# A two-layer diffusion backbone: opening reordered with part of the later keys moved in, last tile split

## The reference

```python
shift, scale, gate = adaln(c, ada_w[i], ada_b[i])        # silu(c) @ ada_w + ada_b, for c and c_ctx
h = rmsnorm(x, norm_w[i]) * (1.0 + scale) + shift         # the same for the context
# layer 0: gated linear attention, 4 heads of 256 keys and 512 values, chunked, in both directions
q, k, v, g = split(h @ w_in, [1024, 2048, 4096])          # 1024 + 1024 + 2048 + 2048 columns
la = log_sigmoid((h @ gate_a1) @ gate_a2 + gate_b) / 16   # decay, for each direction
y = (rmsnorm(o) * silu(g)) @ w_out
# layer 1: differential softmax attention, 8 heads, rotary positions, same shape of gate and output
x = x + gate * y
```

## Time and profile before

| | |
|---|---|
| median of 3 runs | 1578.0 us |
| profiled execution | 1577.87 us, span 1575.9 us |
| TensorE busy | 1545.3 us, 98%, 7602 matmuls |
| VectorE busy | 1161.7 us, 74% |
| ScalarE busy | 607.5 us, 39% |
| TensorE idle in 0 to 180 us, longest | 10.1 (first vectors), 4.7 (context rows), 2.0 (quad 4), 1.7 (remainder of k-tile 4), 1.2 (first w_lo) |
| TensorE idle in 160 to 1576 us | six waits of 0.8 us or less |

### The profile page before, as it was taken

How to read it: one execution, slowest core, us unless ns; L and a number is a source line. 1 busy time by engine, 2 the same in 40 slices (tenths; PEclk the granted TensorE clock), 3 DMA queues, 4 the chain that set the end, 5 groups by cost and what they waited for, 6 DMA issues and landing times.

```text
span 1575.9 us, 19506 instructions
## 1 busy us (share of the span) xinstructions
PE 1545.3 (98%) x7602; PEld 1251.7 (79%) x7602; DVE 1161.7 (74%) x1799; ACT 607.5 (39%) x934; POOL 2.2 (0%) x9
## 2 busy tenths in 40 slices
PE   5999999999999999999999999999999999999998
PEld 3567888788888878888878788888888888888886
DVE  4544878887787789677887787768676868676865
ACT  4222444433444434542232454333343424343642
POOL 0000000000000000000000000000000000000000
PEclk9999999999999999999999999999999999999999
DMA  9996444544544364345776354545445454252554
GB/s 332 363 371 205 131 138 124 186 157 121 168 135 154 113 216 160 108 127 154 251 256 214 95 166 149 177 154 175 143 138 159 136 172 147 94 174 81 162 177 143
DMA packets 177352, 269.02 MB, mean 171 GB/s; under 512 B 12534, under 2 KB 111024, under 8 KB 176588
## 3 DMA queue, kind: packets, MB, share of 16 engines
q1 hardware_dynamic: 170464, 256.55, 51.5%
q10 hardware_dynamic: 6796, 11.22, 2.1%
HBM read 265.60 MB, written 2.12 MB: 170 GB/s over the span
## 4 chain that ended last, share of the span: by engine, by line
PE 87%; DVE 6%; DMA 4%; issue 1%; ACT 1%; SPq 0%; ACTq 0%; DVEq 0%
PE bank L1175 68%; PE bank L1637 5%; DMA ada_w<-in_ada_w 3%; DVE ada_w L1690 3%; PE bank L1351 2%; PE bank L1107 2%; PE bank L1260 1%; PE bank L1261 1%; PE bank L1262 1%; DVE w_lo L1665 1%; DMA u<-in_ctx 1%; PE bank L1407 1%; PE bank L1408 1%; PE bank L1409 1%; PE bank L1589 1%
## 5 line engine op out<-in xcount | busy, mean ns | idle before, releaser
L1175 PE MATMUL bank<-w_lo,acts_hi 128*128 128x512 f32 x1536 | 605.6, 394 | 2.3 <-DVE work L2059 0.8
L1175 PE MATMUL bank<-w_hi,acts_lo 128*128 128x512 f32 x1536 | 598.4, 390 | 0.0
L1175 PE MATMUL bank<-w_hi,acts_hi 128*128 128x512 f32 x1536 | 598.2, 389 | 0.0
L642 ACT ACTIVATE w_hi<-w_raw 128x1024 fp32r<-128x1024 f32 (+1 forms) x296 | 304.7, 1034 | 619.3 <-PE bank L1175 535.5
L1665 DVE TENSOR_TENSOR w_lo<-w_raw,w_hi 128x1024 fp32r<-128x1024 f32 (+1 forms) x296 | 349.8, 1191 | 171.3 <-ACT w_hi L642 170.9
L1175 PEld LDWEIGHTS bank<-w_lo,acts_hi 128*128 128x128 f32 x1536 | 288.4, 188 | 72.7 <-issue 10.2
L1175 PEld LDWEIGHTS bank<-w_hi,acts_lo 128*128 128x128 f32 x1536 | 288.3, 188 | 60.6
L1175 PEld LDWEIGHTS bank<-w_hi,acts_hi 128*128 128x128 f32 x1536 | 288.6, 188 | 57.2
L1690 DVE SCALAR_TENSOR_TENSOR ada_w<-ada_w,silu_p 128x1024 f32<-128x1024 f32 x210 | 261.4, 1280 | 41.0 <-DMA ada_w<-in_ada_w 38.0
L1175 PE MATMUL bank<-acts_hi,w_lo 128*128 128x512 f32 x208 | 83.5, 402 | 2.9 <-DVE acts_lo L1790 1.7
L1175 PE MATMUL bank<-acts_lo,w_hi 128*128 128x512 f32 x208 | 81.6, 392 | 0.0
(11 more groups left out here) (227 smaller groups left out, 1511.1 us busy)
## 6 DMA issues: line engine op xcount, KB each, us to landing
ada_w<-in_ada_w SPq DMA_DIRECT2D x144, 512.0 KB, 4.4
w_raw<-in_diff_w_in SPq DMA_DIRECT2D x256, 256.0 KB, 3.1
w_raw<-in_gla_w_in SPq DMA_DIRECT2D x64, 512.0 KB, 4.3
u<-in_ada_w SPq DMA_DIRECT2D x32, 512.0 KB, 9.6
w_raw<-in_gla_w_out SPq DMA_DIRECT2D x32, 512.0 KB, 4.5
w_raw<-in_diff_w_out SPq DMA_DIRECT2D x32, 512.0 KB, 4.8
w_raw<-in_gla_w_in SPq DMA_DIRECT2D x40, 256.0 KB, 4.0
w_raw<-in_gla_w_in SPq DMA_DIRECT2D x48, 128.0 KB, 3.5
```

Source lines behind the costliest of these rows:

```text
L642: act.activation(w_hi[:, s, :, 0:w], raw[:, s, :, 0:w], ACT.Copy).then_inc(w_hi_ok, 1)
L1175: last = pe.matmul(bank[b][:], a, w, start=(k == 0 and i == 0), stop=(k == NK - 1 and i == 2))
```

## The change

1. Quads 2, 6 and 3 lie in the upper half of `acts_lo` (k-tiles 8 to 15), which is written later, and no longer in `raw`.
2. Pair (0,0) is loaded behind quad 3 and waits for no quad's use. Pairs of the OPEN keys follow behind quad 8. Two new pairs, EARLY, 384 columns wide, follow behind quads 10 and 11: the other key tile of heads 1 to 3, for k-tiles 0 to 3.
3. TensorE's list has a new order: the inverse RMS row ahead of quad 2, the first sum ahead of quad 4, both halves of pair 0 ahead of quads 6 and 7, pair 1 behind quad 8, `early_keys` (3 x 12 products) between quads 13 and 16, `gate_columns` later. VectorE does `low(0, 0)` inside `first_group(0)` and `low(0, 1)` behind `first_group(1)`.
4. The 36 products of `early_keys` are left out of heads 1 to 3: tile 2 of their first chunks starts at k-tile 4, pairs 0 and 1 are 256 columns wide, and VectorE adds the kept part to the result in place of copying it. VectorE copies the three parts out of PSUM, ScalarE moves them to `u`, and one is moved twice.
5. The last pair of weights does tile 0 first, then tile 1. VectorE handles the last tile in two halves of 256 columns; tile 0 and the second half are stored from ScalarE's queue, the first half from SyncE's.

```diff
@@ buffers
-        quad_slot = [ada_w[:, 0], ada_w[:, 1], raw_quads[:, 4:8]] + [u_quads[:, t] for t in range(NT)]
-        quad_slot.append(raw_quads[:, 0:4])
+        lo_quads = nc.alloc_sbuf_tensor_at("lo_quads", [P, 8, CW], F32, offset=lo_at + 4 * 8 * TOK)
+        quad_slot = [ada_w[:, 0], ada_w[:, 1], lo_quads[:, 0:4]] + [u_quads[:, t] for t in range(NT)]
+        quad_slot.append(lo_quads[:, 4:8])
@@ SyncE
-            BEHIND = {5: (0, 0), 7: (0, 1), 9: (OPEN, 0), 10: (OPEN, 1), 13: (0, 2), 14: (0, 3),
+            BEHIND = {3: [(0, 0)], 7: [(0, 1)], 8: [(OPEN, 0), (OPEN, 1)], 10: [(EARLY, 0)], 11: [(EARLY, 1)],
+                      15: [(0, 2)], 16: [(0, 3)], 17: [(OPEN, 2)], 18: [(OPEN, 3)], 20: [(0, 4)], 22: [(0, 5)],
...
-                    if p == 0:
-                        sp.wait_ge(ada_used, 4 if c == 0 else 7)
@@ ScalarE
             group_rows(0)
+            split(0, 0)
             first_highs(0)
-            split(0, 0)
...
                 splits(OPEN, range(2 * g - 2, 2 * g))
+                if g == 1:
+                    splits(EARLY, range(EARLY_PAIRS))
...
+            act.wait_ge(early_out, OPEN_TILES)
+            for i in range(OPEN_TILES):
+                act.activation(early_kept[i], early_part[:, i], ACT.Copy).then_inc(early_copied, 1)
@@ TensorE, project_pair
+                        first = 2 * EARLY_PAIRS if later_head(c) and t == 2 else 0
+                        if k < first:
+                            continue
@@ TensorE, new
+            def early_keys(i):
...
+                b, x = bank[(4, 5, 4)[i]], slice(i * P, (i + 1) * P)
+                for p in range(EARLY_PAIRS):
...
+                    for j in range(2):
...
+                        pe.matmul(b[:], wl, hi[:, k, :], start=(k == 0), stop=False)
+                        pe.matmul(b[:], wh, hi[:, k, :], start=False, stop=False)
+                        last = pe.matmul(b[:], wh, lo[:, k, :], start=False, stop=(k == 2 * EARLY_PAIRS - 1))
@@ TensorE, list of the opening
-            startup_quads(2, 4)
+            inverse_rms_row()
+            startup_quads(2, 3)
             lambda_sums()
-            inverse_rms_row()
+            startup_quads(3, 4)
+            gate_weight_transposes()
+            startup_sum(0)
             startup_quads(4, 5)
-            startup_sum(0)
-            gate_weight_transposes()
+            first_pair(0, range(1))
             startup_quads(5, 6)
-            first_pair(0, range(1))
+            first_pair(0, range(1, 2))
             startup_quads(6, 8)
             startup_sum(1)
-            first_pair(0, range(1, 2))
             startup_quads(8, 9)
-            first_pair(1, range(1))
+            first_pair(1)
             startup_quads(9, 10)
-            first_pair(1, range(1, 2))
             later_keys(0, 0)
-            startup_quads(10, 12)
+            startup_quads(10, 11)
             later_keys(0, 1)
-            gate_columns(range(0, 2))
-            startup_quads(12, 14)
+            startup_quads(11, 12)
             later_keys(0, 2)
+            startup_quads(12, 13)
+            early_keys(0)
+            startup_quads(13, 14)
+            early_keys(1)
             startup_quads(14, 16)
-            gate_columns(range(2, 4))
             startup_sum(2)
+            early_keys(2)
             startup_quads(16, 17)
             first_pair(2)
...
-            gate_columns(range(4, 6))
+            gate_columns(range(0, 4))
...
-            gate_columns(range(6, 8))
+            gate_columns(range(4, 8))
@@ VectorE, first_group
+                if g == 0:
+                    low(0, 0)
                 first_remainder(last)
@@ VectorE, list of the opening
             first_group(0)
-            low(0, 0)
             rows_scaled(range(4, 8))
-            low(0, 1)
-            first_group(1)
-            rows_scaled(range(8, 12))
-            low(OPEN, 0)
-            rows_scaled(range(12, NK))
...
+            rows_scaled(range(8, 10))
+            first_group(1)
+            low(0, 1)
+            rows_scaled(range(10, NK))
+            lows(OPEN, range(2))
             keys_partly(0, 0)
             keys_partly(0, 1)
+            lows(EARLY, range(EARLY_PAIRS))
+            keys_partly(0, 2)
+            early_partly(0)
+            early_partly(1)
             lows(0, range(2, 4))
             first_group(2)
-            keys_partly(0, 2)
+            early_partly(2)
@@ VectorE, heads 1 to 3
+                    elif not first and t == 2:
+                        kept = qkT[:, t] if h == G_HEADS - 1 else early_kept[h - 1]
+                        dve.tensor_tensor(qkT[:, t], bank[t][:], kept, ALU.add).then_inc(freed[t], 1)
@@ tail: TensorE and VectorE
+            def last_output_pair():
...
+                for t in range(2):
...
+                    last.then_inc(acc_ok if t == 0 else last_half, 1)
...
+                for n, (t, first, cols) in enumerate(((0, 0, CW), (1, 0, CW // 2), (1, CW // 2, CW // 2))):
```

More of the change, by code:

```diff
@@ L127, with later_head, width, pieces @@
 ACT_TILES = (9, 11, 13, 15)
-OPEN = -1
+OPEN, EARLY = -1, -2
 OPEN_TILES = G_HEADS - 1
+EARLY_PAIRS = 2
+ORDER = [(c, 2 * g + i) for g in range(PAIRS // 2) for c in ((0, OPEN, EARLY) if g == 0 else (0, OPEN)) for i in range(2)]
+ORDER += [(c, p) for c in range(1, CHUNKS) for p in range(PAIRS)]
+SEQ = {cp: n for n, cp in enumerate(ORDER)}
 def seq(c, p):
[L136 to L148, removed]
+    return SEQ[c, p] if c <= 0 else SEQ[c, 0] + p
+def later_head(c):
+    return 0 < c < OUT0 and c % 3 == 0
+def width(c, p):
+    if later_head(c):
+        return 2 * P if p < EARLY_PAIRS else 3 * P
+    return 3 * P if c < 0 else CW
+def pieces(c, p):
+    if later_head(c):
+        return 1 if p < EARLY_PAIRS else 2
+    if c < 0:
         return OPEN_TILES
-    return 2 if c < OUT0 and c % 3 == 0 or DIFF <= c < OUT1 else 1
+    return 2 if c == 0 or DIFF <= c < OUT1 else 1
 def landed(c, p):
[L156 to L159, removed]
+    return 16 * sum(pieces(*ORDER[n]) for n in range(seq(c, p) % RING, seq(c, p) + 1, RING))
 def open_bank(g, i):
@@ L550, in q_and_k, with parts, early_keys @@
             def q_and_k(h):
-                return side_by_side(wg, h * G_DK, h * G_DK + key0, P if h > 0 else 2 * P)
+                both = side_by_side(wg, h * G_DK, h * G_DK + key0, P if h > 0 else 2 * P)
+                def parts(p, slot):
+                    return both(p, slot)[1:] if h > 0 and p < EARLY_PAIRS else both(p, slot)
+                return parts
+            def early_keys(p, slot):
+                return [(slot[:, :, i * P:(i + 1) * P],
+                         wg[:, 2 * p:2 * p + 2, bass.ds((i + 1) * G_DK + key0, P)]) for i in range(OPEN_TILES)]
             def later_keys(p, slot):
@@ L1166, in project_pair @@
                     for t, b in tiles:
-                        if k == 0 and frees is not None:
+                        first = 2 * EARLY_PAIRS if later_head(c) and t == 2 else 0
+                        if k < first:
+                            continue
+                        if k == first and frees is not None:
                             pe.wait_ge(freed[b], frees(b))
@@ L1174, in project_pair @@
                         for i, (a, w) in enumerate(ops):
-                            last = pe.matmul(bank[b][:], a, w, start=(k == 0 and i == 0),
+                            last = pe.matmul(bank[b][:], a, w, start=(k == first and i == 0),
                                              stop=(k == NK - 1 and i == 2))
@@ L1253, in later_keys @@
                     pe.wait_ge(ada_taken, 4)
+                if g == 1 and i == 0:
+                    pe.wait_ge(early_out, 2)
                 b, x = bank[open_bank(g, i)], slice(i * P, (i + 1) * P)
@@ L1627, in output_pair @@
                 for e in range(2):
[L1628 removed]
+                    k, wh, wl = 2 * kp + e, w_hi[:, seq(OUT1, s) % RING, e], w_lo[:, seq(OUT1, s) % RING, e]
                     if j < 2:
@@ L1640, in output_pair @@
                 last.then_inc(pair_done, 1)
+            def last_output_pair():
+                s = 4 * PAIRS - 1
+                j, kp = out1_pair(s)
+                p = s % PAIRS
+                pe.wait_ge(w_split, seq(CHUNKS - 1, p) + (1 + RING))
+                for t in range(2):
+                    x, out_ = slice(t * P, (t + 1) * P), bank[OUT1_BANKS[j][t]][:]
+                    for e in range(2):
+                        k, wh, wl = 2 * kp + e, w_hi[:, seq(OUT1, s) % RING, e], w_lo[:, seq(OUT1, s) % RING, e]
+                        for i, (a, w) in enumerate(((hi[:, k, x], wl), (hi[:, k, x], wh), (lo[:, k, x], wh))):
+                            last = pe.matmul(out_, a, w, start=False, stop=(e == 1 and i == 2))
+                    last.then_inc(acc_ok if t == 0 else last_half, 1)
             behind_last = {1: key_transposes, 3: query_transposes, 5: attention_scores, 10: weight_transposes,
                            12: attention_outputs, 16: output_transposes}
```

(2 more changed lines are left out.)

72 lines of the change are left out of this document (59 added, 13 removed).

## The result

The changed kernel takes 1586.13 us (median of 7 runs, 1583.4 to 1587.65), the kernel before 1579.02 in its 7 runs beside it (1576.17 to 1581.17). The ratio is 1.0041, 95% interval 1.0032 to 1.0051: slower by 0.41%, about 6.5 us (7.1 by the medians). The forecast was 1577.5, no change that can be told, in a range up to 1581.5. The measured time lies outside it.

A forecast was written before the change was run, and what follows sets the result against it. TensorE's solid row of products bounds the kernel, leaving the opening, one gap and the tail to win. Pair 1 +0.8, clock +1.5, moved products -0.7 and tail -2.1 sum to -0.5: 1577.5 us, range 1572.5 to 1581.5.

The forecast's parts named there:

- First product: Opening: TensorE's first product starts at 36.1 us, 4.2 us earlier, bounds 35.7 and 37.0.
- To the second sum: Opening: with both halves of pair 0 moved ahead, the second sum starts at 47.0 us, before 47.11.
- Where the lead goes: Opening: TensorE idles 3.7 us for VectorE, pair 1 starts at 52.3 against 51.50, a loss of 0.8 us.
- Clock: Opening, behind the 3.7 us idle: one more low-clock stretch costs 1.5 us, bounds 0 and 3.
- The moved products in the opening: 36 products (8.2 us) enter the opening, cover the 1.73 us gap, cost 0.5 for changes and 0.5 for row copy: net -0.7.
- The moved products in the heads: Heads 1 to 3 give back the 8.2 us; other effects there between -0.5 and +1, taken as 0.
- if VectorE holds TensorE in heads 1 to 3: One of the listed signs, in heads 1 to 3, that the forecast is wrong; no size given.
- Tail: Behind the last product: 1.2 us gained on VectorE and 0.9 on the stores, -2.1 in sum, from -1.2 to -2.6.
- Sum: Whole kernel: +0.8 + 1.5 - 0.7 - 2.1 = -0.5, giving 1577.5 us.
- the rivals: Warm throughout 1573.8 (chance 0.22); cold twice 1580.0 (0.15); opening DMA-bound 1567.6 (0.07); no earlier start 1581.5 (0.06).
- the slower one: Opening: low clock holds until 43.4 and returns for two stretches, +2.1: 1580.0, or 1583 with late lows; chance 0.15.

The follow-up runs named there:

- experiment 3: Changed kernel with VectorE's low(0,1) ahead of first_group(1), as before the change: 1582.32 us, ratio 1.0028 to the kernel before.
- 10: experiment 2 and experiment 6 combined, with ScalarE's copy of group 1's row ahead of its split of pair (0,1): 1578.64 us, 1.0000 to the kernel before.
- experiment 5: Changed kernel with 13 extra, never read products in TensorE's wait ahead of pair 1: 1584.42 us, ratio 1.0035 to the kernel before.
- experiment 6: Changed kernel with the second half of pair 0 behind the second sum and low(0,1) ahead of first_group(1): 1582.82 us, 1.0024 to the kernel before.
- Experiment 1: Changed kernel with the 36 early key products put back into heads 1 to 3: 1580.70 us, ratio 1.0008 to the kernel before.
- experiment 2: Changed kernel with the first three half sums one pair of weights later: 1580.88 us, ratio 1.0014 to the kernel before.
- 9: experiment 2 with three VectorE background multiplications moved from head 3's key chunk into its gate chunk: 1576.04 us, 0.9989 to the kernel before.
- 8: experiment 6's start without the moved products, 12 products of a later key moved behind the third sum: 1580.24 us, 1.0013 to the kernel before.
- experiment 13: Kernel before with only the new tail and three VectorE multiplications moved out of head 3's key chunk: 1575.80 us, ratio 0.9985.
- 14: Early start, new order around second sum, six extra products, VectorE's multiplications moved, new tail; no moved products or later sums: 1574.99 us, 0.9975 to kernel before.

## Why the prediction was wrong

Point by point, in its order.

- *First product* at 36.1, bounds 35.7 and 37.0: 37.77, or 36.5 if all of x's 1.3 us are taken off; 35.6 to 37.4 in the other kernels with this start. Right in the mechanism.
- *To the second sum*, 47.0: 48.77, 47.5 on the same footing. Right.
- *Where the lead goes*: a wait of 3.7, pair 1 at 52.3. Measured 3.41, released by w_lo, 53.78 (52.5). Right; experiment 3 shows low(0,1)'s part, and 10 what the other order gives.
- *Clock*: one low stretch of 1.5 us taken, bounds 0 to 3. It came; experiment 5 measures 2.2. Right, undersized by 0.7: only 3 of the first low stretch's 10 us had run under solid products, and I carried these 3 over, but behind this wait products follow at once and run at 0.43 for 4.4 us (53.8 to 58.2). The Trainium skill, "TensorE: Matmul & The Clock Gate", Part 1 (HAM oscillation), says that the burst behind an idle stretch starts at the lower clock. The trace agrees for the wait of 3.41 us, and does not for the one of 2.92 us in head 1, with 1.00 behind it.
- *The moved products in the opening*: gap of 1.73 gone, 0.5 for the row copy (0.72), no quad waited for. Right. (Two readings were a little off, without weight in the sum: 0.79 MB are 2.3 us at 348 GB/s, not 2.1, and the further copy in head 1 is ScalarE's; VectorE has one more in head 3 alone.)
- **The moved products in the heads: the step that failed.** "36 products ... leave heads 1 to 3 and enter the opening: the same sum on a row that is solid on both sides, so nothing by themselves", and for the heads "between -0.5 and +1 ..., and I take 0". Measured: 5.7 us of the 8.2 not given back, in the trace as waits of 2.92, 1.63 and 1.26 ahead of the three half sums. These stand behind the shortened pairs 0 and 1 (behind pair 3 in head 1, right behind pair 1 in heads 2 and 3) and need VectorE's weighed sums and its gated output of the head before. TensorE came 2.7 us (12 x 0.2266) earlier to each; the slack was below nothing in head 1 (0.50 waited before) and 1.1 and 1.5 us in heads 2 and 3 (2.7 less 1.63 and 1.26). Three more kernels that kept the moved products and the places of the sums (3, 5 and 6) show the same three waits, 2.8 to 3.1, 1.3 to 1.5 and 1.3 to 1.5 us. Experiment 1 puts the products back and the waits are gone; 2 moves the sums and gets all back in heads 1 and 2; 9 gets head 3's. My own list had named this as a sign of being wrong, "if VectorE holds TensorE in heads 1 to 3", yet no rival had a price for it. I had read from the earlier trace rows that TensorE loses nothing in the heads. That tells what a wait costs now, not how soon one begins: a solid row may be solid by 1 us. VectorE's 19.16 of 20 us in the same row was the sign, and experiment 2's head 3 shows where it leads.
- *Tail* -2.1: 1.7 in the trace, 2.2 in the runs. Right in sum, in part by luck: from the last product's start to VectorE's end 0.4 us were gained where I had 1.2, and from there to the end 1.3 where I had 0.9. VectorE now starts the last tile 0.5 us behind that start, where before it began the block 0.2 ahead of it.
- *Sum*: the opening was forecast at +1.6, measured +3.8, or +2.5 without x (+1.4 on the mean of three executions each, with 3 us between executions of the same opening); the heads at 0, measured +5.7, of which the 2.0 gained behind head 3 hide a part. The medians differ by 1.3 us more than the two profiled executions (the granted clock of the changed kernel's runs is 0.993 to 0.995). A likely place is the clock behind head 1's wait: it stayed at 1.00 in the changed kernel's profiled execution, which is one of its fastest (three runs took 1583.4 to 1584.2, four 1586.1 to 1587.7), and fell in those of 5 and 6, where chunk 1 to chunk 10 takes 429.7 and 430.2 us in place of 428.0. No slower run was profiled, so this isn't shown.
- Of the rivals, the sign of the slower one came true, but by none of its mechanism: I had looked for it in the opening alone.

## What to carry to other kernels

Work moved off a saturated engine's row is won only if whatever meets that engine next is early by as much: read the slack of each rendezvous behind the place, that is of each point where the engine needs another's result (here three sums, with 0 to 1.5 us), not the engine's busy share. Move the rendezvous with the work, and look which engine is full there. An early start is spent in the same way by in-order queues: a small copy that releases a chain should not stand behind a large one that waits for a transfer (1.8 us lost in experiment 6, 4.5 in 8).

## What was not expected of the hardware

The length of a wait alone did not tell whether the low clock follows. Waits of 1.71 us (experiment 3, 0.60 in 50 to 53 us) and 1.77 (6, 0.50 in 47 to 50) were followed by it, while the 1.73 us ahead of pair 2 in the kernel before was not the earlier trace rows. Nor does the work ahead of the wait settle it: experiment 13 has the same instructions there as the kernel before and the same wait (and 0.56 us more idle at 74.8), and its execution fell to 0.57, where the kernel before has 1.00 in 80 to 84 us; 14, with 1.61 us more idle at 72.5, stayed at 1.00.

```profile
80.46 0.66 PE L1183 MATMUL bank<-acts_hi,w_lo 128*128 128x512 f32 x1 [1.72 <-DVE acts_lo L1813]
...
80.00:84.00 4.00, 3.54 (x9) 2.83 (x10) 3.90 (x9) 2.23 (x4) 0.00 (x0) 0.57 1.09 355
```

The same holds for the 2.9 to 3.1 us in head 1 of the changed kernel, 5 and 6. So a forecast of one low stretch needs a chance beside it, also where the nearest row shows none. 13 extra products in a wait of 3.4 us kept the clock at 1.00 (experiment 5), and made the 24 products behind it 2.2 us faster.
